# The pool stage of two stacked blocks: the band matrix on ScalarE's queue, and its scaling ahead of the second tile's squares

## The reference

```
h = rmsnorm(x, norm_mixer[0])                 # x * rsqrt(mean(x*x) + eps) * gain
for group g, window in enumerate((2, 4, 8, 16)):      # 256 channels each
    d[t] = mean of h over the last `window` tokens - h[t]
y = d @ pool_w[g]                             # 256x256 for each group
x = x + y * pool_scale
```

## Time and profile before

| | us |
|---|---|
| median of 3 runs | 1120.54 |
| lowest and highest | 1120.51, 1120.81 |
| the profiled execution | 1121.29 |
| its span in the profile | 1118.9 |

### The profile page before, as it was taken

How to read it: one execution, slowest core, us unless ns; L and a number is a source line. 1 busy time by engine, 2 the same in 40 slices (tenths; PEclk the granted TensorE clock), 3 DMA queues, 4 the chain that set the end, 5 groups by cost and what they waited for, 6 DMA issues and landing times.

```text
span 1118.9 us, 16758 instructions
## 1 busy us (share of the span) xinstructions
PE 1107.7 (99%) x6429; PEld 963.2 (86%) x6429; DVE 789.5 (71%) x1032; ACT 539.2 (48%) x709; POOL 97.1 (9%) x184
## 2 busy tenths in 40 slices
PE   8999999999999999999999999999999999999997
PEld 7888888898888888888998888888899988888886
DVE  6866666767667666678886676666778867766675
ACT  5533333455654333336785543333456755333332
POOL 2000000000000000001660000000036400000000
PEclk9999999999999999999999999999999999999999
DMA  8865565673358556655963465557489444655551
GB/s 258 266 207 191 177 211 189 216 239 113 116 173 278 190 184 200 210 176 145 268 200 118 165 226 188 187 187 217 144 203 264 134 146 161 213 190 187 187 187 37
DMA packets 175974, 211.21 MB, mean 189 GB/s; under 512 B 24467, under 2 KB 159187, under 8 KB 175922
## 3 DMA queue, kind: packets, MB, share of 16 engines
q1 hardware_dynamic: 166146, 202.89, 56.8%
q0 software_dynamic: 9776, 7.62, 3.7%
HBM read 201.98 MB, written 1.16 MB: 182 GB/s over the span
## 4 chain that ended last, share of the span: by engine, by line
PE 96%; DVE 1%; issue 1%; ACT 0%; DMA 0%; POOL 0%; SPq 0%; DVEq 0%; POOLq 0%; ACTq 0%
PE bank L1643 26%; PE bank L1647 14%; PE bank L1617 13%; PE bank L1618 13%; PE bank L1619 13%; PE bank L1721 4%; PE bank L1929 2%; PE bank L1950 2%; PE bank L1656 1%; PE bank L1787 1%; PE bank L1960 1%; PE bank L1682 1%; PE bank L1713 1%; PE bank L1659 1%; PE bank L1964 1%
## 5 line engine op out<-in xcount | busy, mean ns | idle before, releaser
L688 ACT ACTIVATE whi<-raw 128x2048 fp32r<-128x2048 f32 (+2 forms) x180 | 342.0, 1903 | 387.3 <-PE bank L1647 244.9
L1016 DVE TENSOR_TENSOR wlo<-raw,whi 128x2048 fp32r<-128x2048 f32 x175 | 398.2, 2278 | 145.1 <-ACT whi L688 144.7
L1643 PE MATMUL bank<-h_both,whi 128*128 128x512 f32 x1280 | 304.6, 390 | 0.0
L1643 PEld LDWEIGHTS bank<-h_both,whi 128*128 128x128 f32 x1280 | 237.7, 188 | 47.8
L1617 PE MATMUL bank<-whi,o_hi 128*128 128x512 f32 (+1 forms) x452 | 177.4, 392 | 0.0
L1618 PE MATMUL bank<-wlo,o_hi 128*128 128x512 f32 (+1 forms) x452 | 176.0, 389 | 0.0
L1619 PE MATMUL bank<-whi,o_lo 128*128 128x512 f32 x448 | 174.4, 389 | 0.0
L1647 PEld LDWEIGHTS bank<-h_both,wlo 128*128 128x128 f32 x1280 | 164.1, 191 | 6.2
L1647 PE MATMUL bank<-h_both,wlo 128*128 128x256 f32 x1280 | 166.0, 283 | 0.0
L1617 PEld LDWEIGHTS bank<-whi,o_hi 128*128 128x128 f32 x452 | 85.1, 188 | 17.6 <-issue 1.3
L1619 PEld LDWEIGHTS bank<-whi,o_lo 128*128 128x128 f32 x448 | 84.1, 188 | 17.9
(11 more groups left out here) (202 smaller groups left out, 1330.3 us busy)
## 6 DMA issues: line engine op xcount, KB each, us to landing
raw<-in_w_gate_up SPq DMA_DIRECT2D x44, 1024.0 KB, 5.1
raw<-in_w_down SPq DMA_DIRECT2D x44, 1024.0 KB, 4.9
raw<-in_w_gate SPq DMA_DIRECT2D x22, 1024.0 KB, 5.4
raw<-in_w_up SPq DMA_DIRECT2D x22, 1024.0 KB, 5.3
raw<-in_w_in SPq DMA_DIRECT2D x18, 1024.0 KB, 6.7
raw<-in_w_o SPq DMA_DIRECT2D x12, 1024.0 KB, 4.9
raw<-in_w_kv SPq DMA_DIRECT2D x8, 1024.0 KB, 5.4
raw<-in_w_q SPq DMA_DIRECT2D x4, 1024.0 KB, 5.2
```

The source lines that it names most:

```text
L688: act.activation(whi[:, s, 0:w], raw[:, s, 0:w], ACT.Copy).then_inc(hi_ready, 1)
L1016: dve.tensor_tensor(wlo[:, s, 0:w], raw[:, s, 0:w], whi[:, s, 0:w].bitcast(F32), ALU.subtract).then_inc(lo_ready, 1)
L1643: pe.matmul(bank[bk + jj][:, :], hi[:, kc, jj * P:(jj + 1) * P], h_both[:, kc, :, :].rearrange("p a t -> p (a t)"), start=(kc == 0), stop= ...
```

## The change

Two moves. The load of the band leaves SP's list, and ScalarE issues it, behind its first small activation and ahead of the squares. And on VectorE the scaling of the band for tile 0 stands ahead of the half square of tile 1 instead of behind it. No instruction is added or taken away. The whole diff:

```diff
@@ SP
             sp.dma_start(gain_rows, GAIN_SRC[0].rearrange("(k p) -> k p", p=P)).then_inc(gains_in[0], 16)
-            sp.dma_start(band, c["c_band"].rearrange("p g n -> p (g n)")).then_inc(band_in, 16)
             pool_w = raw[:, 0, :].rearrange("p (g k n) -> p (g k) n", g=4, k=2)
@@ ScalarE
             act.activation(junk[:, 0:T], o_lo[:, 0, :].bitcast(F32), ACT.Square).then_inc(warmed, 1)
             act.wait_ge(warmed, 1)
+            act.dma_start(band, c["c_band"].rearrange("p g n -> p (g n)")).then_inc(band_in, 16)
             for t in range(TT):
                 square(0, t, 0, 2)
@@ VectorE
             second_half_square(0)
             dve.wait_ge(last_square, 1)
             mean_square(0, 0)
+            scaled_band(0)
             second_half_square(1)
-            scaled_band(0)
             dve.wait_ge(last_square, 2)
             mean_square(0, 1)
             scaled_band(1)
```

## The result

The changed kernel takes 1122.28 us (median of 22 runs), the kernel before 1120.61 us (22 runs beside them): the ratio is 1.0016, with a 95% interval of 1.0009 to 1.0023. It is slower by 1.7 us, where 0.4 us faster was forecast, and it lies just outside the range. (A ratio given here is not always the quotient of the two medians.)

A forecast was written before the change was run, and what follows sets the result against it. TensorE was taken as the bound, busy 1107.7 of 1118.9 us, with an early wait for the band. A 0.67 us gain less 0.27 for a later transpose gave 0.40: 1120.54 - 0.40 = 1120.1 us, range 1119.0 to 1122.1.

The forecast's parts named there:

- when the band lands: Band's load issued from ScalarE: forecast to land at 6.6 us instead of 8.2, sharing transfer time with tile 1 of x.
- The bounds that I gave (5.8 to 9.5): Band's landing: 5.8 us from tile 0's issue-to-landing time, up to 9.5 if it stands behind what SP queued.
- 0.67: Most us an earlier band could win: start of band matmuls from 8.92 to 8.25, where TensorE's zeros end.
- The issue costs ScalarE 0.43 us in idle time: ScalarE's added issue after its warm-up activation: taken as 0.4 us, costing nothing because ScalarE idles until its first square at 4.17.
- The transposes and their zeros as cover: TensorE ahead of the band matmuls: gains' rows transpose at 6.63, five multiplications by zero until 8.21, limiting any earlier start.
- That the transpose would move to 6.9: Gains' rows transpose on TensorE: 0.27 us later because tile 1 lands later, cutting the gain to 0.40 us.
- Start at B + 0.65 from the landing B: First tile's band matmuls: start about 0.65 us after the band lands, including VectorE's scaling of 0.56 us.
- Second tile ready at B + 2.93: VectorE's second scaling after the swap: done 2.93 us after the band lands; hidden at 6.6, costing for landings over 7.5.
- The path behind 13.5 us that carries a shift over whole: TensorE from the first weight matmul at 13.52: a shift of less than 0.77 us passes whole into the total.
- The pool weights left at 9.5: First half of the pool weights: landing left at 9.5 us, capping the gain at about 0.5 to 0.6 us.
- the second rival: Band lands no earlier and the swap costs: 1120.8 us, or 1122.1 for a landing at 9.5; chance 0.18.

The follow-up runs named there:

- the move alone: The kernel before with the band issued on ScalarE's queue but VectorE's old order kept: 1122.11 us against 1120.66, ratio 1.0018.
- the version with ScalarE first: The changed kernel, but the band is issued as ScalarE's very first instruction, five zeros kept behind the transpose: 1122.63 us against 1120.92 for the kernel before.

## Why the prediction was wrong

The step that failed is **when the band lands**. I put its landing at 6.6 us, by letting it share the way with tile 1 of x alone and leaving the pool weights out of the sum, although I had let these run beside the band when I reckoned their own landing. Both halves of that are refuted. Tile 1 shared nothing: it landed at 5.9, and the band moved nothing before 5.5. The pool weights, issued at 2.08 and so ahead of the band's 2.49, flowed first and then beside it. It landed at 9.1 and 9.3 (8.8 in the move alone); with the weights held back it lands at 6.8. That this is near my 6.6 is in part luck, since it came about behind tile 1 and not beside it. The bounds that I gave (5.8 to 9.5) held the landing; the value taken from between them didn't.

The second mistake is one of reading. The whole argument went by one trace whose execution was 0.75 us above the median. I took this as a constant to be subtracted, but it was the very wait in question: the two traced executions of before differ by 1.04 us in time and by 1.08 us in the start of the first weight matmul. In the execution of 1120.25 us the band lands at 7.2, the zeros end at 6.24 + 1.59 = 7.83 and the band matmuls start at 7.84, so they stand right behind one another and there was nothing to win, not 0.67. No trace is of the kernel before at its median of 1120.6. The nearest is the version with only the identity and the small tables moved, at 1120.63 us: its band lands at 7.7, its band matmuls start at 8.38 and its first weight matmul is at 12.98, half way between the 12.44 and 13.52 of the two traces of before. By that, 0.5 us was the most that an earlier band could win at the median (an estimate, from 12.98 against 12.44).

Point by point. The issue costs ScalarE 0.43 us in idle time: right, its first square waits for tile 0 all the same. The transposes and their zeros as cover: right as a mechanism, and it showed itself in the version with ScalarE first, where they set the start at 9.89. That the transpose would move to 6.9 was wrong: it is at 6.17. Start at B + 0.65 from the landing B: right, 9.1 gave 9.76. Second tile ready at B + 2.93: right, 11.85 for 9.1, which is B + 2.75. The path behind 13.5 us that carries a shift over whole: right, +2.10 at the first weight matmul and +2.0 at the end. The pool weights left at 9.5: their first half lands at 9.6 and at 8.8 in the two traces of the changed kernel, and it never was what the start waited for. The clock wasn't in the sum: where it falls it adds about 0.9 us at the first weight matmul, and the traced execution with the fall ended 1.4 us later than the one without.

So it was the second rival, on its far side: its price of 1.6 us and 1122.1 us for a landing at 9.5 is close to the 1122.28 measured. That closeness is partly luck. The band landed at 9.1 to 9.3, for which the rival's own sum gives 1.2 to 1.4 us, and it counted from the 8.92 of the longer execution; against the shorter one the loss is 2.0. What it got wrong besides is its division: the swap, which that rival named as the cost, takes about 0.2 to 0.4 us, and the late landing takes the rest. I gave it 0.18, because I reckoned a second queue to free the band of some of what is ahead of it, and forgot that it also frees all that was behind it.

## What to carry to other kernels

In this kernel the band's place in SP's queue protected it in part from what was issued later (5.1 and 6.1 us to landing, 4.6 with nothing behind it). In a second queue, issued 0.4 us later, it had no such place (6.3 to 6.8 against 4.3), while issued at the very start from that queue it needed 4.6 to 4.7 us, and the tiles of x and the gains' rows paid for it. So before a load is moved to another queue while the DMA engines are full, count the bytes in flight on all queues until it lands, also those issued after it. And before a wait of a microsecond is reckoned with, see whether it is there in more than one execution: the distance of the profiled execution from the median may be that wait.

## What the hardware showed unexpectedly

The same transfer of 320 KB, issued at the same time by the same kernel, took 5.1 us to land in one execution and 6.1 in another. It took 4.6 us with nothing issued behind it, and 4.3 from ScalarE's queue.

ScalarE's queue moved nothing for three microseconds after its issue at 2.49, while SP's moved x; with the weights held back it was still two, and SP's queue then moved x too. No run here explains this.

After a stall of 1.2 to 2.3 us of TensorE its granted clock fell to 0.50 for two microseconds and more in some executions. In others it did not: the changed kernel has both (a fall after 2.26 us, none after 2.03), and 2.55 us brought none in the version with the weights held back on SP. The multiplications by zero ran slowly at a granted clock of 1.00 after a wait of 1.32 us: five took 2.50 us instead of 1.43. No run here explains this.
